# MoE expert products: from split float32r over the whole array to plain fp32 in column groups, with a ring of sixteen weight halves

## The reference, cut to what matters

```
logits = hf @ w_router + b_router;  top_val, top_idx = top_k(logits, 4);  wts = softmax(top_val)
per expert e (32 of them), for the tokens that chose it:
    gu = xb @ w_gu[e] + b_gu[e]                       # (rows, 1024) @ (1024, 1024)
    gt = minimum(gu[:, :512], 7);  up = clip(gu[:, 512:], -7, 7)
    act = gt * sigmoid(1.702 * gt) * (up + 1)
    y   = act @ w_down[e] + b_down[e]                 # (rows, 512) @ (512, 1024)
x = x + g2 * sum over a token's 4 experts of weight * y;  out = rms_norm(x, final_g)
```

## Time and profile before

| | before |
|---|---|
| median of 3 runs | 1056.94 us |
| profiled execution | 1057.93 us |
| its span | 1056.1 us |
| first bias matmul of expert 0 | 415.98 us into the span |
| first bias matmul of expert 31 | 1009.10 us |
| TensorE busy | 996.8 us (94%) |
| VectorE busy | 778.8 us (74%) |
| ScalarE busy | 559.8 us (53%) |
| chain that ended last | 90% on TensorE |

### The profile page before, as it was taken

How to read it: one execution, slowest core, us unless ns; L and a number is a source line. 1 busy time by engine, 2 the same in 40 slices (tenths; PEclk the granted TensorE clock), 3 DMA queues, 4 the chain that set the end, 5 groups by cost and what they waited for, 6 DMA issues and landing times.

```text
span 1056.1 us, 13850 instructions
## 1 busy us (share of the span) xinstructions
PE 996.8 (94%) x4523; PEld 671.3 (64%) x4523; DVE 778.8 (74%) x1121; ACT 559.8 (53%) x840; POOL 215.2 (20%) x237
## 2 busy tenths in 40 slices
PE   3889999999999987899999999999999999999995
PEld 2566666667787557666666666666666666666652
DVE  0374967535534555898898898889989889898885
ACT  6334454452223233755575666756666665766742
POOL 1223931105100012212211212121122221212110
PEclk9899999999999998999999999999999999999998
DMA  9826624512316456889899999999999999999745
GB/s 343 297 81 239 239 81 168 188 43 70 118 69 239 159 206 235 307 310 316 307 332 370 360 370 366 351 373 359 369 357 354 377 354 363 368 365 363 245 126 195
DMA packets 63213, 283.35 MB, mean 268 GB/s; under 512 B 7489, under 2 KB 8797, under 8 KB 38601
## 3 DMA queue, kind: packets, MB, share of 16 engines
q1 hardware_dynamic: 53528, 257.93, 65.4%
q0 software_dynamic: 9648, 24.94, 8.9%
HBM read 272.62 MB, written 18.56 MB: 276 GB/s over the span
## 4 chain that ended last, share of the span: by engine, by line
PE 90%; DVE 5%; ACT 2%; issue 1%; DMA 1%; POOL 0%; ACTq 0%; SPq 0%; DVEq 0%
PE ps L1843 33%; PE ps L1578 19%; PE ps L1903 10%; PE ps L1897 9%; PE ps L1777 2%; PE ps L1607 2%; PE ps L1788 2%; PE ps L1626 2%; PE ps L1814 2%; PE ps L1692 2%; PE ps L1821 1%; PE ps L1864 1%; PE ps L1877 1%; DVE attn L1425 1%; DMA X<-in_x_dram 1%
## 5 line engine op out<-in xcount | busy, mean ns | idle before, releaser
L1843 PE MATMUL ps<-whl,xhl 128*96 128x512 f32 x1536 | 369.0, 399 | 0.0
L1307 DVE TENSOR_TENSOR whl<-ring,whl 128x1024 fp32r<-128x1024 f32 x256 | 304.4, 1221 | 52.5 <-ACT whl L965 51.8
L1843 PEld LDWEIGHTS ps<-whl,xhl 128*96 128x96 f32 x1536 | 249.8, 163 | 108.3 <-issue 0.2
L965 ACT ACTIVATE whl<-ring 128x1024 fp32r<-128x1024 f32 x256 | 268.2, 1061 | 63.7 <-PE ps L1843 43.9
L1578 PE MATMUL ps<-h_hi,wb_hl 128*128 128x512 f32 x384 | 127.1, 404 | 1.2 <-POOL wb_hl L652 1.2
L1903 PE MATMUL ps<-X,attn 128*96 128x512 f32 x256 | 115.4, 593 | 0.0
L733 POOL DMA_INDIRECT moe_rows<-mix,ius x31 | 46.3, 1493 | 304.8 <-ACT WC L1034 153.1
L1897 PE MATMUL ps<-whl,ahl 128*96 128x512 f32 x384 | 98.8, 407 | 2.9 <-DVE whl L1307 2.9
L1578 PEld LDWEIGHTS ps<-h_hi,wb_hl 128*128 128x128 f32 x384 | 72.9, 190 | 22.4 <-issue 5.2
L1307 DVE TENSOR_TENSOR whl<-X,whl 128x1024 fp32r<-128x1024 f32 x64 | 78.3, 1225 | 8.9 <-ACT whl L965 8.1
L965 ACT ACTIVATE whl<-X 128x1024 fp32r<-128x1024 f32 x64 | 67.8, 1062 | 20.0 <-PE ps L1843 20.0
(11 more groups left out here) (251 smaller groups left out, 1178.5 us busy)
## 6 DMA issues: line engine op xcount, KB each, us to landing
ring<-in_w_gu_dram SPq DMA_DIRECT2D x128, 1024.0 KB, 10.5
X<-in_w_down_dram SPq DMA_DIRECT2D x64, 1024.0 KB, 10.4
ring<-in_w_ada_dram SPq DMA_DIRECT2D x12, 2048.0 KB, 11.9
ring<-in_w_in_dram SPq DMA_DIRECT2D x6, 2048.0 KB, 7.8
ring<-in_w_out_dram SPq DMA_DIRECT2D x2, 2048.0 KB, 7.9
X<-in_x_dram SPq DMA_DIRECT2D x1, 2048.0 KB, 8.1
ring<-in_w_b_up_dram SPq DMA_DIRECT2D x1, 2048.0 KB, 14.8
ring<-in_w_a_up_dram SPq DMA_DIRECT2D x1, 2048.0 KB, 8.0
```

The source lines that it names most:

```text
L965: nc.scalar.activation(whl[:, buf, 0, :], part, ACT.Copy).then_inc(hi_ok, 1)
L1307: v.tensor_tensor(whl[:, buf, 1, :], part, whl[:, buf, 0, :], ALU.subtract).then_inc(lo_ok, 1)
L1843: last = mm(ps[0:slots, half, :], xhl[:, a, k, :], whl[:, at, b, half * CH:(half + 1) * CH], start=False, stop=(k == KD - 1 and a == 1))
```

## The change

- **Products.** Nothing is split: `xhl`, `ahl` and `whl` are gone, with the ScalarE copies (L965) and VectorE subtractions (L1307, L1388, L1394) that filled them. Every chunk is multiplied as plain fp32. The 96 slots are cut into 64 and 32 (`SA`, `SB`). For the first 64, two matmuls of 512 columns go to the two column groups of 64, each with half of the 1024 output columns. For the last 32, four matmuls of 256 columns go to the four column groups of 32, each with a quarter. So a chunk is six matmuls again: 64x512 twice, then 32x256 four times.
- **Activation.** The up product now lies on all 128 partitions, in three chunks of 128 columns for gate and for up, so the vector steps are 128x384 where they were 96x512, and `turn_act` makes three transposes of 128x128 where there were four of 96x96. Weighing is six instructions in place of two.
- **Weights.** Sixteen half places in eight homes form one ring for w_gu and w_down (`half_home`). Three homes are new (`area_b`, `hT`, `area_a`). A place is refilled when the matmuls that read it are done (`half_used`). SP issues the first two halves earlier, and sixteen in all before the first refill. A w_down load is now two runs of 4 KB for each partition, where it was one of 8 KB.
- **Loops.** TensorE's and SP's loops are unrolled over eight experts where it was two.

The cut diff:

```diff
-HK = KD // 2
-KFR = 2
-NG = 4
-SEQ = KD + KFR
+SA, SB = 64, SLOTS - 64
+NH = 16
+RUN = 8
+PER = 6
...
-        late = sb("late", [P, 4, T])
-        xhl = sb("xhl", [P, 2, KD, slots], F32R)
-        ahl = sb("ahl", [P, 2, KFR, slots], F32R)
-        whl = sb("whl", [P, NG, 2, D], F32R)
...
-        up1 = mix[0:slots, 3584:4096]
-        th = attn[0:slots, 512:1024]
-        av = attn[0:slots, 1024:1536]
-        actT = attn[:, 1536:1536 + KF * slots].rearrange("p (k s) -> p k s", k=KF)
+        up1, th, av = (t.rearrange("p (c q) -> p c q", c=3) for t in
+                       (mix[:, 3584:3584 + 3 * P], attn[:, 512:512 + 3 * P], attn[:, 1024:1024 + 3 * P]))
+        actT = attn[:, 1536:1536 + 3 * P].rearrange("p (c s) -> p c s", c=3)
+        by_chunk = ps[:, 0:2, :].rearrange("p b n -> p (b n)")[:, 0:6 * P].rearrange("p (c u q) -> p c u q", c=3, u=2)
+        gates, ups = by_chunk[:, :, 0, :], by_chunk[:, :, 1, :]
+        b3_of = maskb[0:3 * NE, 0:512].bitcast(BF16).rearrange("p (u g c q) -> p g c u q", u=2, g=2, c=2)
+        late = small[:, :].rearrange("p (a t) -> p a t", a=4)
...
+            dn = w_down[0, bass.ds(e, 1), :, :].rearrange("a (k p) n -> p (a k) n", k=KF)
+            return dn[:, 2 * q:2 * q + 2, :]
...
+        homes = [area_b[:, :], ring[slot_of[NFP - 3]], ring3[:, :], ring[slot_of[NFP - 2]], ring[slot_of[NFP - 1]],
+                 hT[:, :, :].rearrange("p k t -> p (k t)"), X[:, :, :].rearrange("p c d -> p (c d)"), area_a[:, :]]
+        Yin = homes[0].rearrange("p (c d) -> p c d", c=C)
+        res = homes[1].rearrange("p (c d) -> p c d", c=C)
+        def half_home(n):
+            return homes[n % NH // 2][:, (n % 2) * PAIR:(n % 2 + 1) * PAIR]
...
+            def refill(e, r):
+                for q in range(4):
+                    sp.wait_ge(half_used, up_no(e, q) - NH + 1)
+                    load_up(e, q, r * PER - 2 + q)
+                for q in range(2):
+                    sp.wait_ge(half_used, down_no(e - 1, q) - NH + 1)
+                    load_down(e - 1, q, r * PER + 2 + q)
...
-            def hi_part(n, buf, part):
-                if not isinstance(n, int) or n >= NG:
-                    act.wait_ge(granule_used, n - NG + 1)
-                nc.scalar.activation(whl[:, buf, 0, :], part, ACT.Copy).then_inc(hi_ok, 1)
...
-            def rows_high(e):
+            def rows_copy(e, b):
                 act.wait_ge(tx_done, e + 1)
-                nc.scalar.activation(xhl[:, 0, 0:4, :], turned(4), ACT.Copy)
-                nc.scalar.activation(xhl[:, 0, 4:8, :], turned(5), ACT.Copy).then_inc(xh_ok, 1)
+                nc.scalar.activation(chosen[:, b:b + 1], sel3[:, bass.ds(e, 1)], ACT.Copy)
+                nc.scalar.activation(xgT[:, :, :], turned(4), ACT.Copy).then_inc(xg_ok, 1)
...
-            def lo_part(n, buf, part):
-                dve.wait_ge(hi_ok, n + 1)
-                v.tensor_tensor(whl[:, buf, 1, :], part, whl[:, buf, 0, :], ALU.subtract).then_inc(lo_ok, 1)
...
+            def weigh(b, done):
+                for g in range(2):
+                    sl = slice(g * CH, (g + 1) * CH)
+                    v.scalar_tensor_tensor(out=Y[0:SA, b, sl], in0=ps[SA * g:SA * (g + 1), 2, :], scalar=WC[0:SA, b:b + 1],
+                                           in1=g2b[0:SA, sl], op0=ALU.mult, op1=ALU.mult)
+                for j in range(4):
+                    sl = slice(j * 2 * P, (j + 1) * 2 * P)
+                    last = v.scalar_tensor_tensor(out=Y[SA:slots, b, sl], in0=ps[SB * j:SB * (j + 1), 3, 0:2 * P],
+                                                  scalar=WC[SA:slots, b:b + 1], in1=g2b[SA:slots, sl],
+                                                  op0=ALU.mult, op1=ALU.mult)
+                last.then_inc(done, 1)
...
+            def biases(b):
                 pe.wait_ge(b3_ok, 1)
-                mm(ps[0:slots, half, :], sel3[:, bass.ds(e, 1)].broadcast_to([3 * NE, slots]), b3[:, half * CH:(half + 1) * CH],
-                   start=True, stop=False)
-            def up_whole(e, done):
-                for half in range(2):
-                    biases(e, half)
-                    for k in range(KD):
-                        last = mm(ps[0:slots, half, :], xgT[:, k, :], gu_part(0, k)[:, half * CH:(half + 1) * CH], start=False,
-                                  stop=(k == KD - 1))
-                    last.then_inc(done, 1)
-            def up_parts(e, parity, lo, hi):
-                if lo == 0:
-                    for half in range(2):
-                        biases(e, half)
-                for k in range(lo, hi):
-                    pe.wait_ge(lo_ok, up_at(e, k) + 1)
-                    at = up_buffer(e, parity, k)
-                    for a, b in ((0, 0), (0, 1), (1, 0)):
-                        for half in range(2):
-                            last = mm(ps[0:slots, half, :], xhl[:, a, k, :], whl[:, at, b, half * CH:(half + 1) * CH],
-                                      start=False, stop=(k == KD - 1 and a == 1))
-                    last.then_inc(granule_used, 1)
+                for g in range(2):
+                    mm(ps[SA * g:SA * (g + 1), 0, :], chosen[:, b:b + 1].broadcast_to([3 * NE, SA]), b3_of[:, g, :, :, :],
+                       start=True, stop=False, tile_position=(0, SA * g))
+                for j in range(4):
+                    mm(ps[SB * j:SB * (j + 1), 1, 0:2 * P], chosen[:, b:b + 1].broadcast_to([3 * NE, SB]),
+                       b3_of[:, j // 2, j % 2, :, :], start=True, stop=False, tile_position=(0, SB * j))
+            def up_pair(q, w):
+                w = w.rearrange("p (k u g c q) -> p k g c u q", k=2, u=2, g=2, c=2)
+                for i in range(2):
+                    k = 2 * q + i
+                    for g in range(2):
+                        mm(ps[SA * g:SA * (g + 1), 0, :], xgT[:, k, 0:SA], w[:, i, g, :, :, :], start=False,
+                           stop=(k == KD - 1), tile_position=(0, SA * g))
+                    for j in range(4):
+                        last = mm(ps[SB * j:SB * (j + 1), 1, 0:2 * P], xgT[:, k, SA:slots], w[:, i, j // 2, j % 2, :, :],
+                                  start=False, stop=(k == KD - 1), tile_position=(0, SB * j))
+                return last
...
+            def down_pair(q, w):
+                w = w.rearrange("p (k n) -> p k n", k=2)
+                for i in range(2):
+                    k = 2 * q + i
+                    for g in range(2):
+                        mm(ps[SA * g:SA * (g + 1), 2, :], actT[:, k % 2, SA * (k // 2):SA * (k // 2) + SA],
+                           w[:, i, g * CH:(g + 1) * CH], start=(k == 0), stop=(k == KF - 1), tile_position=(0, SA * g))
+                    for j in range(4):
+                        last = mm(ps[SB * j:SB * (j + 1), 3, 0:2 * P], actT[:, 2, SB * k:SB * (k + 1)],
+                                  w[:, i, 2 * P * j:2 * P * (j + 1)], start=(k == 0), stop=(k == KF - 1),
+                                  tile_position=(0, SB * j))
+                return last
...
+            def came(n, rounds):
+                pe.wait_ge(half_in[n % NH], rounds * 48 + n // NH * 16 + 16)
...
-            def down_parts(e, parity):
-                pe.wait_ge(actT_ok, e + 1)
-                pe.wait_ge(al_ok, e + 1)
-                for i in range(KFR):
-                    pe.wait_ge(lo_ok, down_at(e, i) + 1)
-                    at = down_buffer(e, parity, i)
-                    for a, b in ((0, 0), (0, 1), (1, 0)):
-                        for half in range(2):
-                            last = mm(ps[0:slots, 2 + half, :], ahl[:, a, i, :], whl[:, at, b, half * CH:(half + 1) * CH],
-                                      start=(i == 0 and a + b == 0), stop=False)
-                    last.then_inc(granule_used, 1)
-                pe.wait_ge(down_in[1], e * 16 + 16)
-                for k in range(KFR, KF):
-                    for half in range(2):
-                        last = mm(ps[0:slots, 2 + half, :], actT[:, k, :], down_part(k)[:, half * CH:(half + 1) * CH],
-                                  start=False, stop=(k == KF - 1))
-                last.then_inc(dn_done, 1)
```

More of the change, by code:

```diff
@@ L124, in trunk @@
         WC = sb("WC", [P, 2])
+        chosen = sb("chosen", [3 * NE, 2], BF16)
         iug = sb("iug", [P, 2], U32)
@@ L566, in _ @@
+            for e in range(3, RUN):
+                refill(e, e)
+            with sp.Fori(1, NE // RUN - 1) as i:
+                for r in range(RUN):
+                    refill(i * RUN + r, r)
+            for e in range(NE - RUN, NE):
+                refill(e, e)
+            for q in range(2):
+                sp.wait_ge(half_used, down_no(NE - 1, q) - NH + 1)
+                load_down(NE - 1, q, down_no(NE - 1, q))
             most = sp.value_load(cmaxi[0:1, 0:1], min_val=0, max_val=T)
@@ new lines, in came, with up, down @@
+            def came(n, rounds):
+                pe.wait_ge(half_in[n % NH], rounds * 48 + n // NH * 16 + 16)
+            def up(e, r, rounds=0):
```

(36 more changed lines are left out.)

266 lines of the change are left out of this document (75 added, 191 removed).

## The result

The changed kernel has a median of 1121.66 us over four runs (1119.49 to 1124.99), against 1056.81 us for the kernel before in the same session: a ratio of 1.0612, with a 95% interval of 1.0579 to 1.0644. It is 6.1% slower. The profiled execution took 1124.99 us with a span of 1123.2 us. The one run of the kernel before at 1283.42 us, 21% above its others, is left out of the ratio.

What follows compares the result with a forecast made beforehand. TensorE was taken as the bound, DMA nearly equal. Expert 1 at 431.9 us, thirty experts 623, index matmuls 5.3, transposes 1.0, the end to 1091, then 16.3: span 1107, median 1108 us, 4.8% slower, range 1068 to 1140.

Steps and rivals of the forecast that it cites:

- What bounds the kernel: Steady state: TensorE sets the pace at 18.72 us per expert, DMA is nearly as limiting, removing hidden splitting gains nothing there.
- A chunk, 1.58 us: Up and down products on TensorE: 0.858 and 0.43 us of streams plus exposed loads, two switches and stagger, 1.58 us.
- The rest of an expert, 20.8 us: TensorE outside the chunks: biases 0.55, rows 0.80, activation 0.48 us; with twelve chunks at 18.95, 20.8 us per expert.
- Weights: Weight loads: waits are met, DMA having 20.8 us for 18.7 of work; 4 KB runs cost at worst 0.45 us.
- The start: Expert 0's up product starts at 415.4 us, and after rows, chain and turning expert 1 starts at 431.9.
- The sum: Whole profiled execution: start, thirty experts of 20.8 us, index matmuls, weight transposes and end give a span of 1107 us.
- The end: From expert 31's start at 1061 us: up, down(30), turning, copy, down(31) and weighing, reaching 1091 us.
- The final products: What follows the last weighing: unchanged from the kernel before, 16.3 us.
- A: Rival: no switch cost between column groups of 64 and 32; DMA then decides, about 1000 us, 5% faster; chance 0.11.
- C: Rival: the two column groups of 64 don't run beside each other; each chunk gains 0.86 us, 1440 us; chance 0.04.
- B: Rival: the switch costs half; chunk 1.48 us, expert 19.5 us, 1068 us in all; chance 0.07.

Runs made afterwards that it cites:

- The experiment with other banks: Changed kernel with the last expert's down product and weighing in the two banks that the turned rows had: 1115.56 us, ratio 1.0551 to the kernel before.
- whole products: Changed kernel with all 64-wide matmuls of a whole up or down product first, then all 32-wide ones: 1022.72 us, ratio 0.9676 to the kernel before.
- the unrolled kernel: Changed kernel with 64-wide before 32-wide matmuls over each whole up or down product, and TensorE's loop written out: 1020.38 us, ratio 0.9627 to the kernel before.

## Why the prediction was right, and where its size was off

The forecast was 1108 us in a range of 1068 to 1140, slower with a chance of 0.81. It came out at 1122, by the mechanism named.

**What bounds the kernel.** Right. Splitting was hidden work: 374 us less on VectorE brought nothing in the steady state, and the removal of the cheaper split passes shows by itself in the kernel without column groups, 3.3 us more per expert.

**A chunk, 1.58 us.** Right to the hundredth (1.578). Starts in a chunk lie 0.48, 0.53, 0.24 and 0.33 us apart, against 0.48, 0.43 + 0.10, 0.24 and 0.21 + 0.10. The rows of other places carried over: groups of 32 columns and row groups of 64 stood in well for column groups of 64. The terms that the prediction had for a turn, 2 x 0.095 for the switches, 0.05 and 0.024 for exposed loads and 0.027 for the stagger, come to 0.291 us; measured are 0.288. The Trainium skill's statement (TensorEngine Tiling (Array Packing), Key Properties) that a change of mode drains the engine agrees with this price, which holds the weight loads that a turn uncovers as well.

**The rest of an expert, 20.8 us.** Right, 20.79. Biases 0.56 (0.55), rows 0.81 (0.80), activation 0.48 (0.48). The activation chain never made TensorE wait in the steady state.

**Weights.** Right: 6.8 us to land in place of 10.8, a DMA share of 0.94 to 0.97, no wait. I had put it at about 0.9. The slower runs of 4 KB cost nothing under this cover; in the faster kernels they show.

**The start.** Expert 1 starts at 431.81 us (431.9 forecast).

**The sum was 16 us short of the profiled span, 1123.2 against 1107.** Against the median it is 14, as the profiled run lay 3.3 us above its median where the forecast had taken 1.0. Three terms:

- Experts 1 to 30 took 637.8 us where I had 629.1. The loop's jump back is 7.4 us of this. Another 1.6 came at expert 1: after a wait of 1.68 us for the activation the granted clock was 0.65 from 434 to 437 us, while in the kernel with TensorE's loop written out it stayed at 1.00 and expert 1 took 21.46 us in place of 23.05. The rest came out 0.3 under. I had counted the unrolling over eight experts as costing nothing, and had not asked how often TensorE's loop still jumps. The kernel before jumps much more often, with a body of two experts (156 matmuls), and twenty-one of its experts last 18.71 to 18.73 us, so none of its rows could give this price; that there was no row was what I should have written down.
- The end, from the start of expert 31 to the final products, took 35.85 us where I had 30.0. This is the term that I mis-sized with the evidence at hand. The sum had 0.6 us between the last turning and down(31), but the wait on `y_ok` ahead of down(31) lets it start only when expert 30 is weighed: 3.46 us between starts. In the steady state the next up product covers that weighing; at the end nothing does. The stop also brought the granted clock down for the start of down(31), to 0.50 until 1098 us. The experiment with other banks gives 5.1 of the 5.9 us back.
- The final products, at first at half clock again after the second wait, took 17.8 us to the end of the span in place of 16.3, 1.5 us. Before, the granted clock over that piece was 0.87, here it is 0.79.

The missed terms are of one kind: pieces that happen once, where an engine stands still and then runs at 1.2 GHz for a while. The repeated part, 30 times 20.8, was exact, so the verdict was no luck: the missed pieces only add to a loss that the repeated part makes by itself.

**Rivals.** A needed a chunk under 1.39 us, C one of 2.4: both excluded by the rows above. B (0.5 of the price) too. A's arithmetic on DMA came true in another kernel, though: whole products bring an expert under DMA's pace. The time lands at 1020 us and not at A's 1000. In the unrolled kernel the last packets of weights move shortly before 991 us into the span, where A has the last landing at 967 to 980, and what follows takes 35 us, where A has 22.4: A's end, too, left out the wait for the weighing of expert 30 (3.18 us idle) and the half clock after it.

## What to carry to other kernels

Column groups of the array pay in full only in long stretches of one width: here a turn from 64 to 32 columns and back costs 0.29 us, two thirds of what one record of 512 fp32 columns takes (0.43), and the same matmuls sorted by width made a change that lost 6% into one that wins 3.2% (3.7% with the loop unrolled). Before freeing an engine, ask whether it paces anything: here TensorE and DMA were both full, so the most that any reordering could bring was the few per cent to DMA's pace. And cost the pieces that happen once by themselves: a jump back over a long body, the last expert without its cover, and the granted clock after each stop made up nearly all of the error.

## What the runs showed of the hardware

- The step between elements of an fp32 moving operand has a price: sixteen records took 3.43 us with a step of 4 bytes, 3.61 with 8 bytes and 7.33 with 16.
- A jump back over a body of 712 matmuls stopped TensorE for 4.33 to 5.05 us in each of the four kernels that have one (4.38 in the changed kernel), after which the granted clock was half. Over bodies of 304 and of 156 matmuls nothing of the kind is seen.
- A stop that the profile gives as issue can be a wait for another engine: 3.19 us of issue ended 0.1 us after VectorE's last weighing step, and went away with the bank that both used.
